# First weight slot loaded and split ahead of x, x split by halves of the features, the fourth slot of a projection asked for when it is used, the causal mask added by VectorE

## The reference

```
proj = x @ w_in                                # first block: x is (512, 1024), w_in (1024, 7168)
x = layer_norm(ALPHA * x + relu(x @ w_up)**2 @ w_down, ln2_g, ln2_b)
s = q_i . k_j + bias(i, j)                     # fox, and two branches of nsa; heads of 64
p = softmax(where(j <= i, s, -1e30))           # causal mask
o = p @ v
```

## Time and profile before

| | |
|---|---|
| time, median of 3 runs | 1632.13 us (1630.31 to 1632.35) |
| profiled execution, its own time | 1631.07 us |
| its span, first to last instruction | 1629.3 us |
| PE busy | 1545.1 us (95%) |
| DVE busy | 869.4 us (53%) |
| ACT busy | 822.6 us (50%) |
| POOL busy | 58.7 us (4%) |
| mean granted clock of TensorE | 0.978 |

### The profile page before, as it was taken

One profiled execution on the slowest core, in us unless ns is written; L12 is line 12 of the kernel. 1 busy time (PEld: TensorE's weight loads), 2 busy tenths in 40 slices (PEclk: granted clock), 3 DMA queues, 4 the chain that ended last, 5 costly groups with the idle time before them and its releaser, 6 DMA issues.

```text
span 1629.3 us, 24391 instructions
## 1 busy us (share of the span) xinstructions
PE 1545.1 (95%) x9988; PEld 996.2 (61%) x9988; DVE 869.4 (53%) x1729; ACT 822.6 (50%) x1207; POOL 58.7 (4%) x133
## 2 busy tenths in 40 slices
PE   5999998999999999999987989999999999899997
PEld 3444485555487467675875636465685755566686
DVE  6733438887436675655664234354546335577732
ACT  4553557777305554545434444455134556577721
POOL 0000000000000000000000000001000000000000
PEclk7999999999999999999997999999999999999999
DMA  5222331121423433322242566401023432100001
GB/s 172 97 97 97 104 104 52 57 73 52 155 78 108 171 104 104 104 91 99 96 72 62 76 92 93 100 27 30 26 78 104 133 106 78 65 2 2 2 27 52
DMA packets 127119, 132.11 MB, mean 81 GB/s; under 512 B 9664, under 2 KB 124096, under 8 KB 126880
## 3 DMA queue, kind: packets, MB, share of 16 engines
q1 hardware_dynamic: 124240, 119.66, 26.4%
q0 software_dynamic: 2768, 10.89, 1.8%
HBM read 128.44 MB, written 2.10 MB: 80 GB/s over the span
## 4 chain that ended last, share of the span: by engine, by line
PE 61%; DVE 6%; ACT 4%; DMA 3%; issue 1%; POOL 0%; ACTq 0%; DVEq 0%
PE bank L597 8%; PE bank L598 7%; PE bank L599 7%; PE bank L640 7%; PE bank L636 4%; PE bank L637 4%; PE bank L638 4%; PE bank L793 3%; PE bank L811 3%; PE bank L784 3%; PE bank L655 2%; DMA wring<-in_even_w_in 2%; DVE wring L1634 2%; PE bank L774 2%; ACT whigh L1138 1%
## 5 line engine op out<-in xcount | busy, mean ns | idle before, releaser
L597 PE MATMUL bank<-xT,whigh 128*128 128x512 f16 (+1 forms) x984 | 375.7, 382 | 21.9 <-DVE wring L1634 21.3
L598 PE MATMUL bank<-xT,whigh 128*128 128x512 f16 (+1 forms) x984 | 375.5, 382 | 0.0
L599 PE MATMUL bank<-xT,wring 128*128 128x512 f16 (+1 forms) x984 | 375.0, 381 | 0.0
L1634 DVE SCALAR_TENSOR_TENSOR wring<-wring,wsc,whigh 128x2048 f16<-128x2048 f32 (+2 forms) x96 | 221.8, 2310 | 160.7 <-ACT whigh L1138 160.3
L1138 ACT ACTIVATE whigh<-wring,wsc 128x2048 f16<-128x2048 f32 (+2 forms) x96 | 189.2, 1971 | 133.3 <-DVE wsc L1584 114.8
L1156 ACT ACTIVATE whigh<-wring 128x2048 bf16<-128x2048 f32 (+2 forms) x96 | 180.1, 1876 | 131.0 <-DMA wring<-in_even_w_in 47.0
L597 PEld LDWEIGHTS bank<-xT,whigh 128*128 128x128 f16 (+1 forms) x984 | 96.7, 98 | 141.4 <-issue 21.2
L599 PEld LDWEIGHTS bank<-xT,wring 128*128 128x128 f16 (+1 forms) x984 | 96.8, 98 | 117.9 <-issue 3.0
L598 PEld LDWEIGHTS bank<-xT,whigh 128*128 128x128 f16 (+1 forms) x984 | 96.7, 98 | 116.0 <-issue 4.9
L636 PE MATMUL bank<-whigh,slab 128*128 128x256 f16 x512 | 140.3, 274 | 3.9 <-DVE wring L1634 3.9
L637 PE MATMUL bank<-wring,slab 128*128 128x256 f16 x512 | 140.4, 274 | 0.0
(11 more groups left out here) (275 smaller groups left out, 2312.5 us busy)
## 6 DMA issues: line engine op xcount, KB each, us to landing
wring<-in_w_in SPq DMA_DIRECT2D x28, 1024.0 KB, 5.0
wring<-in_w_up SPq DMA_DIRECT2D x16, 1024.0 KB, 5.3
wring<-in_w_down SPq DMA_DIRECT2D x16, 1024.0 KB, 4.8
wring<-in_even_w_in SPq DMA_DIRECT2D x16, 1024.0 KB, 9.3
wring<-in_odd_w_in SPq DMA_DIRECT2D x14, 1024.0 KB, 4.9
wring<-in_w_a SPq DMA_DIRECT2D x4, 1024.0 KB, 4.8
wring<-in_w_out SPq DMA_DIRECT2D x4, 1024.0 KB, 4.8
wring<-in_even_w_out SPq DMA_DIRECT2D x4, 1024.0 KB, 5.2
```

The lines of the kernel that those rows point to most:

```text
L597: pe.matmul(bank, wh[:, k, wcol:wcol + width], xh[:, k, :], start=k == 0, stop=False)
L598: pe.matmul(bank, wh[:, k, wcol:wcol + width], xl[:, k, :], start=False, stop=False)
L599: mm = pe.matmul(bank, wl[:, k, wcol:wcol + width], xh[:, k, :], start=False, stop=k == KC - 1)
L1634: dve.scalar_tensor_tensor(low_of(i)[:, :, 0:m], wring[:, i % NSLOT, :, 0:m], wsc[:, n:n + 1], whigh[:, n % NHIGH, :, 0:m], ALU.mult, ALU. ...
```

## The change

It has four parts.

1. Start: SP asks for slot 0 before x. On DVE `measure(0)` goes before the maximum of x tile 2 and `low(0)` before that of x tile 3; the weight's inverse scale is multiplied by that of x later, in one instruction more. On ACT `high(0)` goes before x. POOL takes the maximum of slot 0 before that of x. ACT and DVE split x in the order of the feature halves (the four pieces of features 0 to 511 first), and PE begins its first tile after four pieces and waits for the other four in the middle of it.
2. `tok_and_norm`: PE asks for slot 3 only before tile 9.
3. `add_and_norm`: all four `first_stats` go behind `low` of slot 3.
4. `attention`: the mask matmuls are gone from PE. DVE adds a float32 "future" block (0, or 1e30 above the diagonal) to the diagonal block of both heads, in PSUM in place, one instruction for each query tile of a step, waits for that to be written, and then takes the minimum as before.

```diff
-                            (future in four bf16 blocks)          future = sb("future", [P, 4, P], BF16)
+                            (one float32 block)                   future = sb("future", [P, P])
@@ block.sync
+            sp.dma_start(wring[:, 0, :, :], stream[0][1]).then_inc(w_in[0], 16)
             for t in range(TT):
                 sp.dma_start(res[:, t, :], a["x"][0, t * P:(t + 1) * P, :]).then_inc(x_in[t], 16)
...
@@ tensor, tok_and_norm
-                w2, w3 = slot(name), slot(name)
+                w = [slot(name)]
                 for t in range(TT):
-                    for s, w in enumerate((w2, w3)):
+                    for s in range(2):
                         n = 8 + 2 * t + s
                         pe.wait_ge(s_(name + "_ev"), n_(name + "_ev", n - 3))
-                        tok_tile(name, w, t, src, banks[n % 4][:, 0:SLOTW])
+                        if n == 9:
+                            w.append(slot(name))
+                        tok_tile(name, w[s], t, src, banks[n % 4][:, 0:SLOTW])
@@ tensor, attention
-                        for half in range(2):
-                            for t, c in parts:
-                                for e in range(2):
-                                    r = slice(e * HD, e * HD + HD)
-                                    pe.matmul(scores(i, e)[:, c + t * P:c + (t + 1) * P], future[r, half, :], future[r, 2 + half, :],
-                                              start=False, stop=False)
@@ tensor, start
-            pe.wait_ge(s_("tr0_ev"), n_("tr0_ev", 8))
-            feat("pool", 8, xhalves, SA)
+            pe.wait_ge(s_("tr0_ev"), n_("tr0_ev", 4))
+            w = slot("pool")
+            feat_tile("pool", w, 0, xhalves, SA[0][:, :], second_half=(s_("tr0_ev"), n_("tr0_ev", 8)))
+            feat_tile("pool", w, P, xhalves, SA[1][:, :])
+            feat("pool", 8, xhalves, SA, first=2)
@@ scalar, start
-            for t in range(TT):
-                turned("tr0", ps, t)
             high(0)
+            act.wait_ge(s_("x_scale"), 1)
+            for h in range(2):
+                for t in range(TT):
+                    act.wait_ge(s_("tr0_mm"), n_("tr0_mm", 2 * t + h + 1))
+                    act.activation(xhalves[0][:, 4 * h:4 * h + 4, t * P:(t + 1) * P], ...
@@ vector, add_and_norm
-                        if ln and s == 1 and t >= 1:
-                            first_stats(name, t - 1)
                 low(slot_at(name, 3))
                 if ln:
-                    first_stats(name, TT - 1)
+                    for t in range(TT):
+                        first_stats(name, t)
@@ vector, start
             for t in range(TT):
+                if t == 2:
+                    measure(0)
+                if t == 3:
+                    low(0)
                 dve.wait_ge(x_in[t], 16)
...
             input_scale("tr0")
-            measure(0)
-            for t in range(TT):
-                turned_low("tr0", ps, t)
-            low(0)
+            dve.tensor_tensor(winv[:, 0:1], winv[:, 0:1], xinv[:, 0:1], ALU.mult).then_inc(dve_chain, 1)
+            dve.wait_ge(dve_chain, own(dve_chain))
+            for h in range(2):
+                for t in range(TT):
+                    dve.wait_ge(s_("x_high"), 4 * h + t + 1)
+                    dve.scalar_tensor_tensor(xhalves[1][:, 4 * h:4 * h + 4, t * P:(t + 1) * P], ...
@@ vector, attention
                         dve.wait_ge(s_(n + "_sc"), i + 1)
+                        for t, c in steps[i][2]:
+                            last = bank[:, 2 * (i % SCORE_SLOTS):2 * (i % SCORE_SLOTS) + 2, c + t * P:c + (t + 1) * P]
+                            ins = dve.tensor_tensor(last, last, future[:, :].unsqueeze(1).to_broadcast([P, 2, P]), ALU.add)
+                        ins.then_inc(s_(n + "_mk"), 1)
+                        dve.wait_ge(s_(n + "_mk"), i + 1)
```

More of the change, by code:

```diff
@@ L78, in constants @@
     c["tril_st"] = (s <= t).astype(np.float32)
-    row = np.arange(P) % HD
-    rows_of = np.stack([p[None, :] == (HD * half + row)[:, None] for half in range(2)], 1)
-    later = np.stack([p[None, :] > (HD * half + row)[:, None] for half in range(2)], 1)
-    c["future"] = packed(bf16_bits(np.concatenate([rows_of * 1.0, later * BIG], 1)))
+    c["future"] = ((p[None, :] > p[:, None]) * BIG).astype(np.float32)
     pick = np.zeros((P, 8, P), np.float32)
@@ L151, in build @@
         tril = sb("tril", [P, P])
-        future = sb("future", [P, 4, P], BF16)
+        future = sb("future", [P, P])
         levels = sb("levels", [P, 3, P], U32)
@@ L355, in build @@
             (tril[:, :], cd["tril_st"]),
-            (future[:, :, :].rearrange("p a n -> p (a n)").bitcast(U32), cd["future"]),
+            (future[:, :], cd["future"]),
             (levels[:, :, :], cd["levels"].rearrange("p (l n) -> p l n", l=3)),
@@ L503, in _ @@
             for i, (_, src, n, _) in enumerate(stream):
+                if i == 0:
+                    continue
                 if i >= NSLOT:
@@ L517, in load_gain @@
                 pool.dma_start(dst, src.to_broadcast([P, DM]).rearrange("p (a n) -> p a n", a=2)).then_inc(s_(name + "_gain"), 16)
-            pool.wait_ge(s_("x_max"), 1)
-            pool.partition_all_reduce(xexp[:, 0:1], xmax[:, 0:1], P, RMAX).then_inc(s_("x_all"), 1)
             for n in range(NSPLIT):
+                if n == 1:
+                    pool.wait_ge(s_("x_max"), 1)
+                    pool.partition_all_reduce(xexp[:, 0:1], xmax[:, 0:1], P, RMAX).then_inc(s_("x_all"), 1)
                 if n == 2:
@@ L591, in slot, with feat_tile @@
                 return wring[:, i % NSLOT, :, :]
-            def feat_tile(name, w, wcol, src, bank, width=P):
+            def feat_tile(name, w, wcol, src, bank, width=P, second_half=None):
                 (wh, wl), (xh, xl) = w, src
                 for k in range(KC):
+                    if second_half and k == KC // 2:
+                        pe.wait_ge(*second_half)
                     pe.matmul(bank, wh[:, k, wcol:wcol + width], xh[:, k, :], start=k == 0, stop=False)
@@ L1173, in _ @@
             size_of(0)
-            for t in range(TT):
-                turned("tr0", ps, t)
             high(0)
+            act.wait_ge(s_("x_scale"), 1)
+            for h in range(2):
+                for t in range(TT):
+                    act.wait_ge(s_("tr0_mm"), n_("tr0_mm", 2 * t + h + 1))
+                    act.activation(xhalves[0][:, 4 * h:4 * h + 4, t * P:(t + 1) * P],
+                                   ps[2 * t + h][:, :].rearrange("p (j n) -> p j n", j=4), ACT.Copy,
+                                   scale=xsc[:, 0:1]).then_inc(s_("x_high"), 1)
             size_of(1)
@@ L1619, in measure @@
                     x = input_of(i)
-                    last = scale_of(wexp[:, c], wsc[:, c], winv[:, c], xinv[:, x:x + 1])
+                    last = scale_of(wexp[:, c], wsc[:, c], winv[:, c], xinv[:, x:x + 1] if i else None)
                     if key in QSLOTS:
@@ L1787, in _ @@
             input_scale("tr0")
-            measure(0)
-            for t in range(TT):
-                turned_low("tr0", ps, t)
-            low(0)
+            dve.tensor_tensor(winv[:, 0:1], winv[:, 0:1], xinv[:, 0:1], ALU.mult).then_inc(dve_chain, 1)
[3 more added lines that the diff above has]
+                    dve.wait_ge(s_("x_high"), 4 * h + t + 1)
+                    dve.scalar_tensor_tensor(xhalves[1][:, 4 * h:4 * h + 4, t * P:(t + 1) * P],
+                                             ps[2 * t + h][:, :].rearrange("p (j n) -> p j n", j=4), xsc[:, 0:1],
+                                             xhalves[0][:, 4 * h:4 * h + 4, t * P:(t + 1) * P], ALU.mult,
+                                             ALU.subtract).then_inc(s_("tr0_ev"), 1)
             measure(1)
```

## The result

| | before | after |
|---|---|---|
| time, median | 1631.36 us (4 runs, 1630.31 to 1632.35) | 1616.05 us (4 runs, 1615.45 to 1617.51) |
| profiled execution, its span | 1631.07 us, 1629.3 us | 1615.45 us, 1613.6 us |
| PE / DVE / ACT busy | 1545.1 / 869.4 / 822.6 us | 1527.3 / 900.3 / 825.9 us |
| mean granted clock | 0.978 | 0.985 |

The change makes the kernel faster: ratio 0.9908, 95% interval 0.989 to 0.9925, that is 15.3 us by the medians, where 11.1 were forecast. The sign was right, and so were the mechanisms but for one, the price of the mask on PE; the time lies 1 us under the lower end of the range.

What follows compares the result with a forecast made beforehand. PE, busy 1545.1 of 1629.3 us, was taken as the bound. Start 1.2, dn3 3.2, nsa 6.0 and fox 0.7 sum to 11.1 us off the 1632.1 median: 1621.0 us, range 1617 to 1627.

Steps and rivals of the forecast that it cites:

- The start: Before the first pool matmul: x tile 1 lands at 9.5, PE starts at 22.45 instead of 23.68, gain 1.2 us.
- Rival (c): Start: x tile 1 lands 1.2 or more late, or POOL and DVE lose the saving; 1622.2 to 1624 us, chance 0.12.
- rival (d): First, qf slot lands earlier, dn3 keeps 5.4 us; second, slow stretch after the start shortens; 1618 us, chance 0.12.
- dn3: Tiles 8 and 9 offer 5.4 us; the DMA of qf's first slot caps the gain at 3.2 us.
- The mask on DVE: Additions in PSUM cost 0.425 us each; DVE takes 17.5 us a pair in nsa, PE 17.94 and stays the bound.
- rival (a): In nsa DVE paces mildly, at about 0.45 us or more an instruction; 1624 us, chance 0.25.
- Rival (b): Writing PSUM in place is dear, 0.68 us an addition, so DVE paces nsa throughout; 1636.5 us, chance 0.07.
- The objection: DVE's mask additions: an estimated 65 ns write surcharge on PSUM would put DVE's pair 0.1 above PE's, time 1621.9 us.
- The mask off PE: Removing mask matmuls saves 0.44 us a triple of steps: 7.0 us in nsa and 1.8 in fox.
- The ends: Fill and drain of nsa: only about 0.2 us gained by step 4, and 0.4 us lost in the drain.
- fox: Mask moved to DVE in fox: DVE has room, but only 12 steps pay for the ends; gain 0.7 us.

Runs made afterwards that it cites:

- either half of the edit: Two runs on the kernel before: only the late request of the fourth slot, 1629.23 us; only the first statistics moved behind `low` of slot 3, 1632.0 us.
- the doubled work: The changed kernel with DVE's mask addition done twice, same result: 1640.32 us.
- Half of the mask: The kernel before with two instead of four mask matmuls on PE per diagonal tile, nothing added on DVE: 1629.49 us.
- no mask at all: The kernel before without its mask matmuls and with nothing in their place: 1623.96 us.
- fourth-slot part alone: The kernel before with only slot 3 asked for at its first use and the first statistics behind its `low`: 1628.77 us, ratio 0.9973.
- both orders altered: The changed kernel with `low(0)` behind the scale of x and ACT's size sum for the next key behind the first root: 1615.34 us, later 1613.82 us.
- the parts alone: The kernel before with one part each: start 1628.63 us, slot 3 request with statistics 1628.77 us, mask moved to DVE 1623.44 us.

## Why the prediction was right or wrong

**The start: mechanism right, term too small.** Forecast 1.2 us, measured 2.2 (first pool matmul 21.50 for 22.45). Of the 0.95, 0.8 is the landing of x tile 1: I read "same bytes ahead of it, so the same moment" from the old order, and in every profile with slot 0 first it landed at 8.5 to 8.8. There is more behind it. In the old order the landing of x tile 3 moves from profile to profile, from 9.4 to 10.8 us, and the first pool matmul moves with it, from 23.66 to 25.06, mean 24.0 of eight profiles; with slot 0 first tile 3 lands at 11.1 to 11.4, and in the order of the change PE starts at 21.4 to 21.6. The one profile that I forecast from was among the earliest, so on the mean the start is worth some 2.6 us. The other steps held within 0.1 us. Rival (c), a start that gives nothing, had its place here and fell. The prediction's cover was sized right: the wait for the other four pieces costs nothing, as the half tile outlasts them.

**The stretch behind the start: rival (d)'s second half.** The first 28 matmuls took 7.4 for 9.0 us, since only 6 of them ran at 1.2 GHz (0.43 us each) and not 14. But without the start part these matmuls took 7.4 to 9.0 us too, 8.1 on the mean of eight profiles, and with it 7.4 to 8.2, mean 7.7. So some 0.4 us of it may be the part's; the rest is scatter of the granted clock.

**dn3: right.** Forecast 3.2, measured 3.3 us, with both halves of the reasoning in the trace: 5.7 us gained at tiles 8 and 9 (5.4 forecast), and the DMA of qf's slot, ACT behind it and DVE's reciprocal behind ACT as what is late next. What the prediction did not see is that either half of the edit would have done nearly as well. The first half of (d), the full 5.4, did not come. The reciprocal came at 839.15, 2.3 us ahead of my 841.5, but dn3 as a whole had moved up by that much (819.71 to 817.41).

**The mask on DVE: right.** 0.42 to 0.43 us an addition (forecast 0.425), DVE busy 16.69 of a pair and, by the gaps of the doubled work, 17.36 with gaps (forecast 17.5). PE stays the bound: rival (a) needed 0.45 or more and fell; its decision point is 0.47 by the estimate above. Rival (b) fell: an addition that reads and writes a bank takes 0.43 us, and the old adds of 128x256 that only read one 0.42, so the write side adds 0.01 at most. The objection was an estimate of 65 ns for the write side, the difference between the 125 ns on PSUM and the 60 on SBUF that the Trainium skill gives (Perfetto Trace Analysis, "Optimizing Scalar/DVE Operations"); the trace does not bear it out.

**The mask off PE: the step that failed.** I took the mask's cost from the links L779 of the chain, 0.11, 0.11 and 0.22: 0.44 a triple, 7.0 us in nsa. The true price is 0.56 a triple (a pair 1.12 and not 0.88) and 9.0 us, since each one-tile step also gets 0.056 us back from the q.k matmuls behind the mask, most likely since their first weight load no longer lies open. 1.9 us of the 4.2 us missing in the forecast are here. Half of the mask shows that these 0.056 us go only with the last mask matmul. The ends cost 0.6 us of the 9.0 (1.0 forecast); against no mask at all, which gains 9.6 in nsa, DVE's additions cost 1.3 to 1.7 there.

**fox: nearly nothing.** 0.7 forecast; 1.1 in the first pair of profiles. At equal clock it is 0.2. Windows over the same three stretches, fourth-slot part alone, then both orders altered:

```profile
1057.71:1072.91 15.20, 10.88 (x85) 5.85 (x84) 8.30 (x18) 8.25 (x23) 0.00 (x0) 1.00 0.21 70
1072.91:1091.93 19.02, 19.02 (x195) 13.18 (x195) 11.33 (x26) 12.13 (x41) 0.00 (x0) 1.00 0.00 1
1091.93:1153.82 61.89, 59.73 (x311) 33.44 (x310) 33.38 (x68) 30.76 (x71) 7.40 (x11) 1.00 0.07 20
```

```profile
1050.35:1066.19 15.84, 9.95 (x61) 5.28 (x60) 10.01 (x23) 8.08 (x23) 0.00 (x0) 1.00 0.21 67
1066.19:1084.16 17.97, 17.97 (x167) 12.43 (x166) 14.21 (x35) 12.75 (x41) 0.00 (x0) 1.00 0.00 1
1084.16:1146.24 62.08, 59.29 (x299) 33.09 (x297) 35.05 (x71) 31.09 (x71) 7.37 (x11) 1.00 0.08 20
```

The fill loses 0.64, the middle gains 1.05, the drain loses 0.19.

**The sum.** At equal clock the places give 2.2 + 3.3 + 8.35 + 0.2 = 14.0 us. With the 0.4 behind the start, and the 0.4 that the start is worth more on the mean than in the first pair of profiles, it is 14.8. The medians say 15.3 and 15.7, the parts alone 17.1. The 0.5 to 0.9 us between the places and the medians stays open: it is within the intervals and within what the granted clock moves from profile to profile, and no run here tells whether the change shifts that on the average.

**The range.** It reached down to 1617 for an earlier qf slot and a shorter slow stretch. It had no case for a term of the sum that is itself too small, though the mask's term was read from one kind of row alone. That the time came out beyond (d)'s 1618 is not (d)'s doing: its first half did not come, and its second is 0.4 us.

## What to carry to other kernels

Price a short matmul that is to be removed by the whole iteration, not by its own link in the chain: the matmuls behind it may get shorter with it (here 0.056 us a step, most likely a weight load that lay open). Before an engine is given work, double that work in an experiment, which shows at once how far away the point is at which that engine takes over (here 0.04 us an instruction). And of an edit with two halves run each alone: here either half gave nearly all of dn3's gain.

## What the runs showed of the hardware

- A float32 weight load of 64x128 takes 187 ns here and a bfloat16 one 94. Behind two or four short mask matmuls the q.k matmuls of a one-tile step take 0.91 or 0.70 us, right behind bias matmuls of 512 or 384 columns 0.86 or 0.65.
- VectorE adds 128x256 float32 in place in PSUM in 0.42 to 0.43 us; with one operand there and the result in SBUF it takes 0.41 to 0.42.
- With a megabyte issued ahead of x's four tiles x tile 1 landed at 8.5 to 8.8 us in every profile. The same number of bytes in the other order ended with x tile 3, at 9.4 to 10.8 us: later, and with more scatter.
- With the same instructions, some stretches take 1.2 to 1.9 us more or less from one execution to the next, by the granted clock (1.00 or 0.56 over the same 33 matmuls at 1221 us; 8.6 or 10.5 us at 911 us in the two profiles of before). Comparisons of 1 us need several profiles or the place in the trace.
